# A decoder's last stage: filter spectra of a Hyena mixer from positions split by parity and frequencies in pairs, and the sum and difference of the two directions from stacked products

## What is computed

```python
def hyena_filters(L, w1, b1, w2, b2, w3, freq):          # L = 256
    ...                                                  # emb: 33 features for each of the 256 positions
    hdn = jnp.sin(fr * (emb @ w1 + b1))                  # 256 x 64
    hdn = jnp.sin(fr * (hdn @ w2 + b2))                  # 256 x 64
    h = (hdn @ w3).reshape(L, HY_ORDER, 2, HY_WIDTH)     # 2 orders, 2 directions, 768 channels
    h = h * decay[:, None, None, :]
    h = h / (jnp.sum(jnp.abs(h), axis=(0, 2), keepdims=True) + EPS)
    zero = jnp.zeros((1, HY_ORDER, HY_WIDTH), f32)
    return jnp.concatenate([h[:, :, 0], zero, h[:0:-1, :, 1]], axis=0)

def fft_long_conv(z, kfull):
    L = z.shape[1]
    zf = jnp.fft.rfft(z, n=2 * L, axis=1)
    kf = jnp.fft.rfft(kfull, n=2 * L, axis=0)
    return jnp.fft.irfft(zf * kf[None], n=2 * L, axis=1)[:, :L]
```

## Time and profile before

| | |
|---|---|
| median of 3 runs | 1893.99 us (1892.75 to 1894.63) |
| the profiled execution's own time | 1894.76 us |
| its span in the profile | 1893.0 us |
| PE busy | 1775.0 us, 94% of the span |
| DVE busy | 774.3 us, 41% |
| ACT busy | 309.4 us, 16% |
| granted TensorE clock, mean over the span | 0.97 |

### The profile page before, as it was taken

How to read it: one execution, slowest core, us unless ns; L and a number is a source line. 1 busy time by engine, 2 the same in 40 slices (tenths; PEclk the granted TensorE clock), 3 DMA queues, 4 the chain that set the end, 5 groups by cost and what they waited for, 6 DMA issues and landing times.

```text
span 1893.0 us, 25589 instructions
## 1 busy us (share of the span) xinstructions
PE 1775.0 (94%) x10362; PEld 1120.7 (59%) x10362; DVE 774.3 (41%) x1545; ACT 309.4 (16%) x665; POOL 52.1 (3%) x89
## 2 busy tenths in 40 slices
PE   4999999999999989899999999999999799999998
PEld 3886754444444438688857444444443487768875
DVE  5666422221222126677853222222211457534173
ACT  0111310100000022331131101000000222220121
POOL 0110000000000000000000000000000010010000
PEclk9999899999999989999899999999999899999999
DMA  9977499999999985764484999999999674215301
GB/s 404 356 271 290 173 373 425 425 425 425 425 425 425 426 350 193 260 234 171 162 324 188 395 425 425 425 425 425 425 425 425 266 281 178 88 46 198 119 23 45
DMA packets 82115, 576.86 MB, mean 305 GB/s; under 512 B 9148, under 2 KB 11452, under 8 KB 12800
## 3 DMA queue, kind: packets, MB, share of 16 engines
q1 hardware_dynamic: 70992, 494.65, 63.7%
q0 software_dynamic: 10992, 80.43, 11.4%
HBM read 573.98 MB, written 1.06 MB: 304 GB/s over the span
## 4 chain that ended last, share of the span: by engine, by line
PE 67%; DMA 19%; SPq 6%; DVE 5%; issue 2%; ACT 1%; DVEq 0%
PE ps L335 65%; DMA wbuf<-in_moe_gu 8%; DMA hma<-in_moe_gu 5%; SPq L1403 5%; DMA slab<-in_moe_gu 4%; PE ps L339 2%; DVE hma L551 1%; DMA wP<-in_moe_gu 1%; SPq L1418 1%; DMA slab<-in_ada 0%; DVE slab L2139 0%; ACT slab L342 0%; DVE slab L2958 0%; DVE slab L2955 0%; DMA wbuf<-in_od_out 0%
## 5 line engine op out<-in xcount | busy, mean ns | idle before, releaser
L335 PE MATMUL ps<-slab 128*128 128x128 f32 (+9 forms) x3224 | 551.3, 360 | 13.6 <-DMA slab<-in_moe_gu 9.7
L335 PEld LDWEIGHTS ps<-slab 128*128 128x128 f32 (+4 forms) x3224 | 347.7, 172 | 193.4 <-issue 166.9
L335 PE MATMUL ps<-hma,wbuf 128*128 128x256 f32 (+1 forms) x1520 | 342.6, 386 | 2.2 <-DVE mods L606 1.3
L335 PE MATMUL ps<-wbuf,slab 128*32 128x512 f32 (+3 forms) x1088 | 313.5, 608 | 19.2 <-DMA wbuf<-in_moe_gu 18.9
L335 PEld LDWEIGHTS ps<-hma,wbuf 128*128 128x128 f32 (+1 forms) x1520 | 289.5, 192 | 51.3 <-issue 7.7
L342 ACT ACTIVATE slab<-ps 128x256 f32<-128x256 f32 (+4 forms) x125 | 58.5, 476 | 959.8 <-PE ps L335 950.4
L335 PE MATMUL ps<-hma,slab 128*32 128x512 f32 (+2 forms) x472 | 186.0, 607 | 10.0 <-DMA hma<-in_moe_gu 10.0
L335 PEld LDWEIGHTS ps<-wbuf,slab 128*32 128x32 f32 (+2 forms) x1088 | 96.9, 134 | 160.5 <-issue 121.9
L1621 DVE TENSOR_TENSOR slab<-ps,slab 128x256 f32<-128x256 f32 x44 | 18.7, 425 | 392.3 <-ACT slab L342 392.3
L335 PE MATMUL ps<-slab,cst 128*32 128x512 f32 (+5 forms) x490 | 129.3, 550 | 8.9 <-ACT slab L342 8.9
L551 DVE SCALAR_TENSOR_TENSOR hma<-wbuf,cs,hma 128x1024 f32<-128x1024 f32 x102 | 130.8, 1282 | 7.8 <-DMA wbuf<-in_ada 4.5
(11 more groups left out here) (274 smaller groups left out, 1502.3 us busy)
## 6 DMA issues: line engine op xcount, KB each, us to landing
wbuf<-in_moe_gu SPq DMA_DIRECT2D x89, 1024.0 KB, 24.4
slab<-in_moe_gu SPq DMA_DIRECT2D x71, 1024.0 KB, 20.2
wbuf<-in_ada POOLq DMA_DIRECT2D x60, 1024.0 KB, 5.6
wbuf<-in_moe_d SPq DMA_DIRECT2D x55, 1024.0 KB, 25.8
hma<-in_moe_gu SPq DMA_DIRECT2D x47, 1024.0 KB, 24.0
cst<-in_moe_gu SPq DMA_DIRECT2D x34, 1024.0 KB, 23.2
wbuf<-in_od_in SPq DMA_DIRECT2D x30, 1024.0 KB, 4.8
hma<-in_moe_d SPq DMA_DIRECT2D x25, 1024.0 KB, 25.4
```

The source lines that it names most:

```text
L335: return e.matmul(o, lhsT, rhs, start=start, stop=stop, skip_group_check=skip)
```

## The change

The positions of the filters are put in another order, the even ones into the first half and the odd ones into the second; the tables `emb`, `dec`, `DC` and `DS` are laid out so. The frequencies are put in pairs, k in the first half and 255 - k in the second. For such a pair the even positions give the same cosine and the odd ones the opposite one (for the sine the other way round). So only the products with the first 128 frequencies are made, for the even and for the odd positions apart, each into its own bank, and the second half comes from their difference: 6 units `y_spec` of two products each. ACT takes the odd part out into the place of the second half (`odd_part`), and DVE then makes the sum and the difference from PSUM and that copy (`spectrum_dve`).

The sum and the difference of the directions now come out of the filters' product itself: the hidden values are stacked in 128 partitions, once as they are and once with the lower half negated, against weights whose two directions are stacked as well. A unit of `y_filt` is now (m, q, o, hf) with q for sum or difference. The second product of the small network is made twice, into partitions 0 to 63 and 64 to 127 of its bank, and the second sine is taken in three instructions and two of one column, which set the backward direction's position 0 to zero. The norm uses |F| + |B| = max(|F + B|, |F - B|): ACT takes the absolute values of sum and difference, DVE the larger, and POOL adds the two halves once. The tokens are turned with every second position (a stationary operand with a step of two values) to have the same order. The weights w3 come in one transfer of 128 partitions in place of two of 64.

```diff
     s = np.arange(256)
-    w = (2 * s[None, :] + 1) * np.pi / 512 * s[:, None]
-    for name, m in (("dc", np.cos(w)), ("ds", np.sin(w)), ("dct", np.cos(w).T / 256), ("dst", -np.sin(w).T / 256),
+    split = np.concatenate([s[0::2], s[1::2]])
+    freq = np.concatenate([s[0:128], s[255:127:-1]])
+    w = (2 * freq[None, :] + 1) * np.pi / 512 * s[:, None]
+    for name, m in (("dc", np.cos(w)[split]), ("ds", np.sin(w)[split]), ("dct", np.cos(w).T / 256),
...
             e.wait_ge(*on("y_hd", 0))
-            mm(e, p[0:64, 0:256], hw2, y_hd[:, 0, :], True, True).then_inc(*P.up("y_h2"))
+            for r in (0, 64):
+                t = mm(e, p[r:r + 64, 0:256], hw2, y_hd[0:64, 0, :], True, True)
+            t.then_inc(*P.up("y_h2"))
...
         def sin_act(e, i):
             e.wait_ge(*on("y_sx", i))
-            afn(e, y_hd[:, i, :], y_hd[:, 2, :], ACT.Sin).then_inc(*C.up("y_hd", i))
+            if i == 0:
+                afn(e, y_hd[0:64, 0, :], y_hd[0:64, 2, :], ACT.Sin).then_inc(*C.up("y_hd", 0))
+                return
+            afn(e, y_hd[:, 1, :], y_hd[:, 2, :], ACT.Sin)
+            afn(e, y_hd[0:64, 4, :], y_hd[0:64, 2, :], ACT.Sin)
+            afn(e, y_hd[64:128, 4, :], y_hd[64:128, 2, :], ACT.Sin, scale=-1.0).then_inc(*C.up("y_hd", 1, 0))
+            e.wait_ge(*C.now)
+            afn(e, y_hd[64:128, 1, 0:1], y_hd[64:128, 2, 0:1], ACT.Copy, scale=0.0)
+            afn(e, y_hd[0:64, 4, 0:1], y_hd[0:64, 2, 0:1], ACT.Copy, scale=0.0).then_inc(*C.up("y_hd", 1))
...
         def hyena_pool(e):
-            for i in range(1, 4):
-                e.wait_ge(*on("y_ab", i))
-                e.tensor_tensor(y_ab[0], y_ab[0], y_ab[1], ALU.add).then_inc(*G.up("y_add", i))
+            e.wait_ge(*on("y_mx", 1))
+            e.tensor_tensor(y_ab[0], y_ab[0], y_ab[1], ALU.add).then_inc(*G.up("y_add"))
...
         def filt_dve(e, n):
...
-            if n % 8 == 7:
+            if n in (11, 15):
+                m = n // 12
+                e.wait_ge(*on("y_ab", m, 1))
                 if m == 0:
-                    e.wait_ge(*on("y_ab", 1))
-                    e.memset(y_f[0][1][0:1, :], 0.0).then_inc(*V.up("dve"))
-                e.wait_ge(*V.now)
-                e.tensor_tensor(y_hs[m], y_f[m][0], y_f[m][1], ALU.add)
-                e.tensor_tensor(y_hd2[m], y_f[m][0], y_f[m][1], ALU.subtract).then_inc(*V.up("y_hsd", m))
+                    e.tensor_tensor(y_ad[0:1, :], y_ab[0][0:1, :], y_ad[0:1, :], ALU.add).then_inc(*V.up("dve"))
+                    e.wait_ge(*V.now)
+                e.tensor_tensor(y_ab[m], y_ab[m], y_ad, ALU.max).then_inc(*V.up("y_mx", m))
+
+        def spectrum_dve(e, n):
+
+            q, c = Y_SPEC[n]
+            o = slice(c * 512, c * 512 + 512)
+            k0, k1 = ((y_KR, y_KI)[q][f][:, o] for f in range(2))
+            e.wait_ge(*on("y_Ko", n))
+            if q == 0:
+                e.tensor_tensor(k0, bank("y_spec", n, 0)[:, :], k1, ALU.add).then_inc(*V.up("dve"))
+            else:
+                e.scalar_tensor_tensor(k0, bank("y_spec", n, 0)[:, :], -1.0, k1, ALU.mult, ALU.subtract).then_inc(
+                    *V.up("dve"))
+            e.wait_ge(*V.now)
+            e.tensor_tensor(k1, bank("y_spec", n, 0)[:, :], k1, ALU.subtract).then_inc(*V.up("y_K", n))
 
         def hyena_pe(e):
-            for n, (f, q, c) in enumerate(Y_SPEC):
-                if n == 4:
+            for n, (q, c) in enumerate(Y_SPEC):
+                if n == 3:
                     rstd_pe(e, "yx", hT)
-                p = fill_bank(e, ("y_spec", n), ("y_K", n))
-                e.wait_ge(*on("y_hsd", 1))
+                e.wait_ge(*on("y_fd", 15))
                 for m in range(2):
-                    t = mm(e, p[:, :], (DC, DS)[q][:, m, f * 128:f * 128 + 128],
-                           (y_hs, y_hd2)[q][m][:, c * 512:c * 512 + 512], m == 0, m == 1)
+                    p = fill_bank(e, ("y_spec", n, m), (("y_K", "y_Ko")[m], n))
+                    t = mm(e, p[:, :], (DC, DS)[q][:, m, 0:128], (y_hs, y_hd2)[q][m][:, c * 512:c * 512 + 512], True, True)
...
-                        t = tr(e, p[:, m * 128:m * 128 + 128], y_z[:, j, m * 128:m * 128 + 128])
+                        t = tr(e, p[:, m * 128:m * 128 + 128], y_z[:, j, :].rearrange("p (n m) -> p m n", m=2)[:, m, :])
...
         def hyena_dve(e):
+            for n in range(3):
+                spectrum_dve(e, n)
             rms_dve(e, "yx", xT, 15, 9, hT, lambda i: ("y_res", "r3"), None, hT)
+            for n in range(3, 6):
+                spectrum_dve(e, n)
```

More of the change, by code:

```diff
@@ L119, in shape_constants @@
     e = np.zeros((128, 256))
-    e[:33] = emb.T
+    e[:33] = emb.T[:, split]
     blk["emb"] = e
@@ L2495, in attn_act @@
             ada_row_act(e, 18)
-            for i in range(4):
-                m, dr = i // 2, i % 2
-                e.wait_ge(*on("y_fd", 4 * i + 3))
-                if i > 1:
-                    e.wait_ge(*on("y_add", i - 1))
-                afn(e, y_ab[1 if i else 0], y_f[m][dr], ACT.Abs).then_inc(*C.up("y_ab", i))
+            for m in range(2):
+                e.wait_ge(*on("y_fd", 8 * m + 3))
+                afn(e, y_ab[m], y_hs[m], ACT.Abs).then_inc(*C.up("y_ab", m, 0))
+                e.wait_ge(*on("y_fd", 8 * m + 7))
+                if m:
+                    e.wait_ge(*on("y_mx", 0))
+                afn(e, y_ad, y_hd2[m], ACT.Abs).then_inc(*C.up("y_ab", m, 1))
         def attn_dve(e):
@@ L2664, in build @@
         DC, DS, CT, ST, FC, FS = (pair(K(n)) for n in ("dc", "ds", "dct", "dst", "fc", "fs"))
-        Y_FILT = [(m, dr, o, hf) for m in range(2) for dr in range(2) for o in range(2) for hf in range(2)]
-        Y_SPEC = [(f, q, c) for f in range(2) for q in range(2) for c in range(3)]
+        Y_FILT = [(m, q, o, hf) for m in range(2) for q in range(2) for o in range(2) for hf in range(2)]
+        Y_SPEC = [(q, c) for q in range(2) for c in range(3)]
         Y_CONV = [(s, i) for s in range(3) for i in range(3)]
@@ L2684, in sin_dve @@
                 e.wait_ge(*on("y_hd", 0))
-            ts(e, x, bank(f"y_h{i + 1}")[0:64, 0:256], hyf[0:64, i:i + 1], hyf[0:64, 2:3], ALU.add,
+            ts(e, x, bank(f"y_h{i + 1}")[0:n, 0:256], hyf[0:n, i:i + 1], hyf[0:n, 2:3], ALU.add,
                ALU.mult).then_inc(*V.up(f"y_s{i + 1}"))
@@ L2721, in filt_pe @@
                 e.wait_ge(*on("landed", "w3"))
-            lhs = y_hd[:, 1, m * 128:m * 128 + 128]
-            for a0, a1 in ((c0, min(max(c0, 2048), c0 + 384)), (min(max(c0, 2048), c0 + 384), c0 + 384)):
-                if a1 > a0:
-                    t = mm(e, p[:, a0 - c0:a1 - c0], lhs,
-                           y_w3[:, a0:a1] if a1 <= 2048 else y_w3b[:, a0 - 2048:a1 - 2048], True, True)
-            t.then_inc(*P.up("y_filt", n))
+            mm(e, p[:, 0:384], y_hd[:, (1, 4)[q], m * 128:m * 128 + 128],
+               y_w3[:, o * 768 + hf * 384:o * 768 + hf * 384 + 384], True, True).then_inc(*P.up("y_filt", n))
@@ L2729, in filt_dve @@
         def filt_dve(e, n):
-            m, dr, o, hf = Y_FILT[n]
+            m, q, o, hf = Y_FILT[n]
             e.wait_ge(*on("y_filt", n))
-            if n == 12:
-                e.wait_ge(*on("y_ab", 0))
-            e.tensor_tensor(y_f[m][dr][:, o * 768 + hf * 384:o * 768 + hf * 384 + 384], bank("y_filt", n)[:, 0:384],
+            e.tensor_tensor((y_hs, y_hd2)[q][m][:, o * 768 + hf * 384:o * 768 + hf * 384 + 384],
+                            bank("y_filt", n)[:, 0:384],
                             K("dec")[:, m * 768 + hf * 384:m * 768 + hf * 384 + 384], ALU.mult).then_inc(
@@ L2829, in hyena_act, with odd_part, first_parts @@
         def hyena_act(e):
-            def spectrum(n):
-                f, q, c = Y_SPEC[n]
+            def odd_part(n):
+                q, c = Y_SPEC[n]
                 e.wait_ge(*on("y_spec", n))
-                if n == 3:
-                    e.wait_ge(*on("y_add", 3))
-                afn(e, (y_KR, y_KI)[q][f][:, c * 512:c * 512 + 512], bank("y_spec", n)[:, :], ACT.Copy,
-                    scale=(1.0, -1.0)[q]).then_inc(*C.up("y_K", n))
-            def spectra():
-                for n in range(4):
-                    spectrum(n)
+                afn(e, (y_KR, y_KI)[q][1][:, c * 512:c * 512 + 512], bank("y_spec", n, 1)[:, :], ACT.Copy).then_inc(
+                    *C.up("y_Ko", n))
+            def first_parts():
+                for n in range(3):
+                    odd_part(n)
             e.preload_act_table_set(LN_EXP)
-            rstd_act(e, "yx", xT, hT, eps6, lambda i: ("y_res", "r3"), rs_t[:, 0, 0:256], None, spectra)
-            for n in range(4, 12):
-                spectrum(n)
+            rstd_act(e, "yx", xT, hT, eps6, lambda i: ("y_res", "r3"), rs_t[:, 0, 0:256], None, first_parts)
+            for n in range(3, 6):
+                odd_part(n)
             for n, (s, i) in enumerate(Y_CONV):
@@ L3163, in packed @@
     out["moe_d"] = rows(v["moe_w_down"]).reshape(2, 64 * 128, 2048)
-    out["hy_w3_2"] = v["hy_w3_2"]
```

(1 more changed line is left out.)

23 lines of the change are left out of this document (11 added, 12 removed).

## The result

The changed kernel takes 1875.41 us (median of 4 runs, 1874.82 to 1878.44); the kernel before, run beside it, 1893.37 us (4 runs, 1891.3 to 1894.63). The ratio is 0.9914, with a 95% interval of 0.9897 to 0.993.

A forecast was written before the change was run, and what follows sets the result against it. PE, busy 94% of the span, was taken as the bound. Terms -10.3 - 0.4 + 0.5 + 0.1 + 0.1 + 0.1 = -9.9 us gave 1884.3 us, range 1881.9 to 1887.0 (forecast's own: 1883.2 to 1885.7).

The forecast's parts named there:

- The spectra: From E, the start of the spectra: 24 products of 512 columns become 12, saving 10.3 us on PE.
- DVE and the banks: In the spectra: DVE's six added passes cost 0; the fifth product's wait for its bank, 0 to 1 us, taken as 0.1.
- The wait for `mods`: Second group of four filter units: PE no longer waits for a bank freed by DVE's mods operation, gaining 0.4 us.
- Filter units: 16 units of 384 columns stay; a product's columns cost the same from 128 partitions as from 64, so 0.
- The second `y_h2` product: Small network: its second product, made twice, costs one more product in a run, a loss of 0.5 us.
- The second sine: Small network: ACT's extra operations, 1.0 to 1.3 us, against 1.15 us of cover; loss 0 to 0.2, taken as 0.1.
- The turns: Turning the tokens: 24 turns load with a step of two values; loss 0 to 0.6 us, taken as 0.1.
- The clock: Rival: low clock stretch behind the norm goes, 1.8 us gained (1882.5, chance 0.10), or one more appears, 1.8 lost (1886.1, 0.08).
- the order around the norm is the same: Argument against the rival that the clock falls in other places: instructions around the norm keep their order; no size given.
- small terms of -0.3 to +1.4: Bounds of the small terms about the sum, from which the forecast's own range of 1883.2 to 1885.7 was drawn.

The follow-up runs named there:

- after_two_more: The changed kernel with two more products of 512 columns, read by nobody, ahead of the spectra; 1879.27 us (9 runs), ratio 0.9943.
- before again: The kernel before, unchanged, measured and traced once more; 1889.38 us (12 runs), ratio to itself 0.9992.
- pairs_only: The kernel before with the 12 spectra products by parity and frequency pairs, its filters left at 64 rows; 1881.61 us, ratio 0.9945.
- after_filt64: The changed kernel with filter products made from the lower 64 partitions alone, one direction left out; 1880.0 us (7 runs), ratio 0.9943.
- stack_only: The changed kernel with its stacked filter units but all 24 spectra products as in the kernel before; 1887.46 us, ratio 0.9974.
- after_h2_serial: The changed kernel with both y_h2 products written to partitions 0 to 63, sharing the array's columns; 1881.59 us (one run).
- after_turn_plain: The changed kernel with the tokens turned in blocks of 128 following positions, without the step of two; 1879.1 us (one run).

## Why the forecast was wrong

The direction, the bound and the largest term were right, and the sum was 3.8 us short of the lasting gain: 9.9 against 13.7. The other 4 us of the first measurement are no lasting gain; two thirds of them are seen in the first 1510 us of its two profiles. Term by term:

- *The spectra*, -10.3 from E on, which the list of what the profile would show puts at E + 16.4 to 16.6: measured -10.13 with the wait of the next point in it, and 16.57. Right.
- *DVE and the banks*, 0 and +0.1: the passes of DVE cost nothing. The bank was free at E + 3.43, as forecast, and the wait cost 0.22 us all the same, since there is a handoff of 0.11 us and the load of the weights waits with its product (this is inside the 10.13). POOL's addition ended 0.05 us ahead of `y_res`, so that whether two such passes would hold each other up was not tried.
- *The wait for `mods`*, -0.4: measured 0.42 (the fourth group: 3.19 us with it; 2.59 now, of which 0.18 is the next point). Right.
- *Filter units*, 0: **this step failed.** The prediction said that a product costs the same from 128 partitions as from 64 "as far as these rows tell". The product does, but the change between 64 and 128 rows is not free: 1.7 us over the five groups. The timeline of PEld could have told, where the loads at such borders start only with their products, behind an idle time of 0.17 to 0.55 us; the prediction argues from PE's rows alone.
- *The second `y_h2` product*, +0.5: **mis-sized**, 0.0. I took the price of one more product in a row, without asking which part of the array it uses.
- *The second sine*, +0.1: measured +0.24. ACT's five operations end 1.24 us later with respect to `y_h2`, against the cover of 1.15, and the handoff to PE (DVE ends at 1541.14, PE starts at 1541.29) comes on top. Within 0 to 0.2, nearly.
- *The turns*, +0.1: 0, hidden.
- *The clock*, as a rival with a chance of 0.10 for the loss of the low stretch: it happened, and gives 1.7 us. Its size was right and its chance too small. The prediction's argument against it, that "the order around the norm is the same", is **the second step that failed**: the order was the same in `after_two_more` too, which has the low stretch.

Summed over the stretches this is +0.24 - 0.42 - 1.68 - 10.13 - 1.73 = -13.72 us, all of the lasting difference. Of the 3.8 us that the forecast was short, the two steps that failed are 3.4 and the `y_h2` term is 0.5; the sine and the wait for the bank go the other way. One sum of the prediction does not come out: small terms of -0.3 to +1.4 about 1884.3 give 1884.0 to 1885.7, and not a lower end of 1883.2.

What decides where the clock falls is not settled. The low stretch was there in all four traces with 64-row filters and the norm in one piece (before, before again, `pairs_only`, `after_filt64`) and in none of those with 128-row filters and the norm in one piece but `after_two_more` (the changed kernel three times, `stack_only`, `after_h2_serial`, `after_turn_plain`). Shown is that a shift of 1.5 us brings it back and that the number of spectra is not what removed it (`stack_only`). That the filters' rows act through the time that they take, 1.7 us, is the simplest reading of both, but `after_filt64` changes the rows and the times together. The place of the norm behind `y_h1` supports it. With 12 products for the spectra the norm starts 169.36 to 169.77 us behind `y_h1` in the five traces without the low stretch and 170.86 to 171.22 in the three with it, `after_two_more` among them. With 24 products it starts at 179.45 without (`stack_only`) and at 181.35 and 181.36 with it (the kernel before, twice). Where `y_h1` itself starts, anywhere from 1507.66 to 1514.00, makes no difference. By the Trainium skill (TensorE: Matmul & The Clock Gate, What's actually happening) the place varies from run to run; here it varied from run to run near the start of the program and was the same in each repeated trace behind the norm.

## What to carry to other kernels

Read the weight loads' row beside the products': a load that starts only with its product, at a change of the shape of the weights, is PE time, and filling the array's rows removes it even where the products get no shorter. Idle time of PEld alone does not tell: between the spectra's loads it is 0.24 us each time and costs nothing. A product that is added on free columns of the array can be free, so price it by where it lies and not by its size. And compare two profiles from a landmark just ahead of the change: a difference of whole programs of 1.9 ms carried 3 to 4 us here of spread that has nothing to do with it.

## What was not expected of the hardware

- A product whose bank comes free just when it would start still comes 0.22 us late: its weights are loaded only then, 0.11 us behind the end of the reader.
- A group of float32 products of 64 rows between products of 128 rows costs 0.39 us of PE at its two borders, whether it has two products or four (50.01 against 48.35 us over five groups).
- Two products of 64 x 64 with 256 columns from the same rows into different columns of the array take 0.58 us together, as long as one, and 1.00 us on the same columns.
- A step of two float32 values in a stationary operand adds 0.01 us to a load (1.59 against 1.47 us for twelve).
- Behind 2.6 us of one-column products the granted clock falls to half for 3.4 us, or not at all, and this hangs on 1.5 us of work ahead of them. The fall costs 1.6 to 1.9 us.
- The first 1510 us of the same instructions took 1507.66 to 1514.00 us in different executions, with a mean granted clock of 0.93, 0.98 or 0.99 between 100 and 150 us. Why an execution gets one or the other is open.
